# The two layers of a fused encoder trunk as a loop of two rounds, with the layer's number in a register

## What is computed

```python
def trunk_layer(x, pos, lw, lb, past):
    cq, ckv_raw, kr_raw, hq, hf, hi, hg, cu, cv, ga, gb, gc = jnp.split(x @ lw['w_in'], idx, axis=-1)
    ...   # A: latent attention; B: HGRN2 recurrence; C: gated MLP over chunks of 128 tokens
    m = jax.nn.sigmoid(ga) * y_a + jax.nn.sigmoid(gb) * y_b + jax.nn.sigmoid(gc) * y_c
    x = layer_norm(ALPHA * x + m @ lw['w_o'], lw['ln1_g'], lw['ln1_b'])
    gate, up = jnp.split(x @ lw['w_up'], 2, axis=-1)
    x = layer_norm(ALPHA * x + (jax.nn.silu(gate) * up) @ lw['w_down'], lw['ln2_g'], lw['ln2_b'])
    return x, (ckv, krope, S_fin, v_cm)
```

## Time and profile before

| | |
|---|---|
| median of 3 runs | 2124.44 us |
| lowest and highest | 2120.12, 2127.49 us |
| the profiled execution | 2126.03 us, its span 2124.2 us |
| TensorE busy | 2079.7 us, 98% |
| VectorE, ScalarE, GpSimd busy | 1175.1 us (55%), 713.6 us (34%), 82.7 us (4%) |
| mean granted TensorE clock | 0.987 of 2.4 GHz |
| DMA | 164.46 MB, mean 77 GB/s |

### The profile page before, as it was taken

The page is one execution under the profiler, slowest core; times in us unless marked ns, Lnnn a source line. Parts: engine busy times, 40 slices in busy tenths (PEclk is TensorE's granted clock), DMA queues, the critical chain, the costliest instruction groups (busy, mean ns, idle before and its releaser), DMA issues.

```text
span 2124.2 us, 38406 instructions
## 1 busy us (share of the span) xinstructions
PE 2079.7 (98%) x15974; PEld 1999.2 (94%) x15974; DVE 1175.1 (55%) x1886; ACT 713.6 (34%) x1154; POOL 82.7 (4%) x87
## 2 busy tenths in 40 slices
PE   7999999999999999999999999999999999999996
PEld 5899998898999999999989999989889999999996
DVE  5435645674376666654454366366725766666436
ACT  4232134444343232222343211354433432322224
POOL 1000001000010000000010000010000200000001
PEclk9999999999999999999999999999999999999997
DMA  5232213221132233322233222132213232332231
GB/s 168 80 81 54 67 44 84 70 62 51 51 109 80 79 89 89 87 84 83 85 90 81 70 61 72 43 93 57 66 31 100 80 89 80 89 89 81 85 93 52
DMA packets 288147, 164.46 MB, mean 77 GB/s; under 512 B 8712, under 2 KB 279280, under 8 KB 288016
## 3 DMA queue, kind: packets, MB, share of 16 engines
q1 hardware_dynamic: 284368, 153.11, 25.7%
q0 software_dynamic: 3168, 8.33, 1.3%
q10 hardware_dynamic: 480, 1.13, 0.2%
HBM read 157.88 MB, written 4.66 MB: 77 GB/s over the span
## 4 chain that ended last, share of the span: by engine, by line
PE 95%; DVE 3%; ACT 1%; issue 0%; DMA 0%; DVEq 0%; ACTq 0%
PE acc L669 51%; PE acc L655 25%; PE ring L689 4%; PE ring L773 2%; PE ring L916 2%; PE ring L935 1%; PE acc L689 1%; PE ring L924 1%; PE ring L986 1%; PE ring L968 1%; PE ring L1138 1%; PE ring L810 0%; PE ring L800 0%; DVE y L1807 0%; PE ring L903 0%; PE ring L824 0%
## 5 line engine op out<-in xcount | busy, mean ns | idle before, releaser
L1299 ACT ACTIVATE whi<-raw 128x1024 fp32r<-128x1024 f32 (+6 forms) x342 | 314.2, 919 | 751.7 <-PE acc L669 422.4
L1807 DVE TENSOR_TENSOR wlo<-raw,whi 128x1024 fp32r<-128x1024 f32 (+6 forms) x342 | 357.3, 1047 | 298.3 <-ACT whi L1299 297.0
L669 PE MATMUL acc<-xh,whi 128*128 128x272 f32 x1440 | 324.9, 307 | 2.9 <-DVE tmp L1807 2.6
L669 PE MATMUL acc<-xh,wlo 128*128 128x272 f32 x1440 | 300.2, 290 | 0.0
L669 PE MATMUL acc<-xl,whi 128*128 128x272 f32 x1440 | 299.9, 290 | 0.0
L655 PE MATMUL acc<-xh,whi 128*128 128x274 f32 (+1 forms) x1408 | 294.4, 290 | 0.0
L655 PE MATMUL acc<-xh,wlo 128*128 128x274 f32 (+1 forms) x1408 | 292.6, 289 | 0.0
L655 PE MATMUL acc<-xl,whi 128*128 128x274 f32 (+1 forms) x1408 | 292.2, 289 | 0.0
L669 PEld LDWEIGHTS acc<-xh,whi 128*128 128x128 f32 x1440 | 229.1, 191 | 18.7 <-issue 13.8
L669 PEld LDWEIGHTS acc<-xl,whi 128*128 128x128 f32 x1440 | 229.1, 190 | 0.0
L669 PEld LDWEIGHTS acc<-xh,wlo 128*128 128x128 f32 x1440 | 228.2, 190 | 0.0
(11 more groups left out here) (373 smaller groups left out, 3120.2 us busy)
## 6 DMA issues: line engine op xcount, KB each, us to landing
raw<-in_w_in_dram SPq DMA_DIRECT2D x106, 512.0 KB, 3.7
raw<-in_w_up_dram SPq DMA_DIRECT2D x88, 512.0 KB, 3.7
raw<-in_w_down_dram SPq DMA_DIRECT2D x32, 512.0 KB, 3.8
raw<-in_w_o_dram SPq DMA_DIRECT2D x16, 512.0 KB, 3.8
raw<-in_w_down_dram SPq DMA_DIRECT2D x16, 384.0 KB, 3.3
raw<-in_w_pc_dram SPq DMA_DIRECT2D x16, 256.0 KB, 2.8
raw<-in_w_pb_dram SPq DMA_DIRECT2D x16, 256.0 KB, 2.8
raw<-in_w_pa_dram SPq DMA_DIRECT2D x16, 256.0 KB, 2.8
```

Source lines behind the costliest of these rows:

```text
L669: last = pe.matmul(dst[:, b * 512:b * 512 + HALF], w[:, c:c + P], x[:, k0 + a, b * HALF:(b + 1) * HALF], start=start and a == 0 and q == 0 ...
L1299: return act.activation(dst, src, ACT.Copy)
L1807: return dve.tensor_tensor(out, a, b, op)
```

## The change

Every engine's walk over the layers becomes a loop on the chip with two rounds, whose counter `l` is a register. The body is built once. What depends on `l` (the wait values, the addresses of weights and outputs, the column of `lbcol`) is worked out by register instructions. The lines that count a semaphore's events in the first layer alone, and the reset of TensorE's buffer numbers, go, since the body is written only once. The norm keeps its place. In the changed file the lines stand about 10 higher: L1299 is L1288 there, L1807 is L1796, L689 is L679, L816 is L806.

```diff
-    first_layer = [True]
-
-    def layers():
-
-        for l in range(DEPTH):
-            first_layer[0] = l == 0
-            yield l
-        first_layer[0] = True
-
     def inc(name, times=1):
-        if first_layer[0]:
-            used[name] = used.get(name, 0) + times
+        used[name] = used.get(name, 0) + times
         return S_(name), (16 if name in DMA_SEMS else 1)
...
-        for l in layers():
+        with sp.Fori(0, DEPTH) as l:
             for n in range(2, 4):
                 load(l, U_CV + n, raw3(n, 2, 512), w_in[l, :, 2 * n:2 * n + 2, C_CV:C_CV + 512])
...
-        for l in layers():
-            ngroup[0] = ntile[0] = 0
+        with pe.Fori(0, DEPTH) as l:
             token_major(l, U_CV, "cv")
...
-        for l in layers():
+        with act.Fori(0, DEPTH) as l:
             for n in range(1, 4):
                 next_hi(l, n + 1)
...
-        for l in layers():
+        with dve.Fori(0, DEPTH) as l:
             dve.wait_ge(S_("lb_max"), 4)
...
-        for l in layers():
+        with pool.Fori(0, DEPTH) as l:
```

## The result

The changed kernel took 2131.94 us (median of 11 runs, 2128.18 to 2138.57), the kernel before 2124.70 us (median of 11 runs, 2120.12 to 2130.47). The ratio is 1.0035, with a 95% interval of 1.0022 to 1.0049: slower by 0.35%, where 2131 us had been forecast. The profiled execution took 2133.86 us, its span 2132.3, which is 8.1 us longer than the span before.

The account below looks back on a forecast made before the run. TensorE, busy 2079.7 of 2124.2 us, was taken to bound the kernel. Register form 0.5, new wait 3.2 and lower clock 2.5 made +6.2 us on the 2124.4 median: 2131 us, range 2124 to 2140 (8 in 10).

Parts of the forecast that it names:

- B: Layer border: ScalarE's jump back (3.0 us) and added table load (1.28 us) make TensorE wait 3.2 us at its third unit.
- the prediction's sign: ScalarE's trace shows a hole of about 3 us behind the last `xh` copy, then table load, then high part.
- rival 1: Layer border: jump hidden, ScalarE's program running ahead or block still held; 2125.6 us, not slower; chance 0.12.
- What the prediction called hidden: Layer border: TensorE's jump within its 3.8 us idle gap, VectorE's before unit 2's high part; SyncE, GpSimd delays covered.
- rival 4: Layer border: instruction fetch takes 5 to 7 us, adding +2 to +4 us, 2133 to 2136; chance 0.08.
- C: Behind the new wait at the third unit: TensorE's clock falls to its lower level, +2.5 us, from 0 to 5.1.
- A: Inside both layers: waits and addresses from registers change 22 hops ending TensorE's waits, +0.5 us, from -1.3 to +2.2.

Follow-up runs that it names:

- the last experiment: Kernel before, both layers written out, second layer leaving out the splits only a next layer needs: 2117.37 us against 2124.18, ratio 0.9971.

## Why the prediction was right

**B, the jump: right in kind and size.** ScalarE's jump was taken for 3.0 us and measured 2.8 to 2.9 (the changed kernel, and ScalarE alone in the loop); the chain to the third unit was worked out as a wait of 3.2 us and measured 3.4. Idle ScalarE was for 2.1 us only, where the prediction's sign was a hole of about 3: its 3.0 us count from the start of the last copy. That the wait came so near is in part luck, since two small errors nearly cancel: from the start of the last `xh` copy to the third unit it took 6.5 us in place of 6.7, and TensorE was ready for it after 3.1 us in place of 3.5. Three runs tie it to the far jump: the short loop (0.51 us a round), ScalarE alone (same hole, an instruction packet inside it), and the unit moved ahead of the jump (wait gone).

The rule of the Trainium skill, "Runtime: NRT & Kernel Launch", instruction fetch, on a taken branch to a page that isn't held, agrees with that. The queue rule behind rival 1, from the Trainium skill, "Advanced Engine Details and Errata", queue depths, didn't hide the jump. The instruction packet starts 1.0 us after the start of the last `xh` copy in the changed kernel (at 1075.98), not two copies sooner, since each of these copies waits for the norm. With unit 2's copy in between it starts 1.1 us after the same copy. So the part of rival 1 by which ScalarE's program runs ahead of its work is true, but only up to the next wait that isn't met.

What the prediction called hidden was hidden: on TensorE (its gap didn't grow), on SyncE and GpSimd. On VectorE it was hidden behind ScalarE's chain only: by itself it makes a wait of 2.7 us. The prediction's price of 3.0 us implied 1.7 of it (1080.4 + 0.2 + 1.2 = 1081.8, against 1080.14), but its text didn't say so. (In rival 4, +4 us gives 2135 and not 2136; nothing hangs on it.)

**B, the table load: right, but of less weight than its 1.28 us.** Without it the wait fell by 0.5 us in the traces, since VectorE's jump comes next.

**C, the clock: right in kind, its size by luck.** Taken as 2.5 us, it was 2.7 in the profiled execution. But four traces have such a wait, of 2.7 to 4.0 us, and the six microseconds behind it show 0.52 in the changed kernel and the following in the others (ScalarE alone; all but ScalarE; no table load):

```profile
1079.40:1085.40 6.00, 6.00 (x19) 0.72 0.68 179
...
1080.70:1086.70 6.00, 6.00 (x26) 1.00 0.83 242
...
1080.50:1086.50 6.00, 6.00 (x26) 1.00 0.78 229
```

The two longer waits (3.4 and 4.0) were followed by low clock, the two shorter (2.7 and 2.9) not, and neither were the waits of 1.2 us of the table load alone and of the short loop. The loss was 2.7 us once, 1.7 once (0.28 of 6 us, ScalarE alone) and twice nothing. With one trace each it stays open whether the length decides it or where the wait falls against earlier low stretches. The runs of the changed kernel themselves aren't alike: four of the eleven show a mean granted clock of 0.988 and take 2128.2 to 2128.7 us, six show 0.985 and take 2131.5 to 2133.9 us.

**A, the register form: small, but over the term.** With TensorE, SyncE and GpSimd in it the ratio is 0.9991, with all five and the jump hidden 0.9998; the intervals reach from -0.22% to +0.14%, so the times can't tell A's 0.5 us from 0. The stream of the up loop is as before:

```profile
656.53 260.59 PE acc L645 x2058
```

The traces, matched matmul by matmul, show more than 0.5: TensorE falls back by 0.7 us in layer 0 (599 to 650) and 0.9 in layer 1 (1601 to 1690), the largest steps being at the first unit of `w_o` (0.2) and at the first up unit (0.3). It is 1.6 us together in the changed kernel and with the unit moved ahead as well, 1.4 with all but ScalarE in the loop, 0.4 with TensorE, SyncE and GpSimd in it, and 0.2 with ScalarE alone. So most of it needs VectorE's register form. 1.6 us is inside the range of -1.3 to +2.2, but not by its working: that had looked at hops that end TensorE's waits, and these lie at places where TensorE hadn't waited before.

**The sum.** 0.5 + 3.2 + 2.5 = 6.2 us was forecast. The medians differ by 7.2 us, and by 6.1 between the changed kernel and the one with the unit moved ahead, each against its own runs of before; that one is B and C, less what the useless split of the last round costs. In the two traces A 1.6, B 3.5 and C 2.7 make 7.8 of the 8.1 us. So the sum came right with A taken too low and C near by luck; the term that carries it, B, was right.

## What to carry to other kernels

Here a jump back over a whole layer cost ScalarE and VectorE about 3 us each, and a short one 0.5 us or less. So before you write such a loop, read on every engine what its first work in the body feeds, and how late that may be. Where it is short of 3 us, put one more unit of look-ahead in front of the jump; where two engines are short of it, both need that. The time counts from the last wait ahead of the jump that isn't met yet, and work behind that wait runs beside the jump, as ScalarE's did with the unit moved ahead. And ask what the last round does for a round that never comes: here that was worth as much as the jump.

## What the runs showed that I had not expected

- The price of the far jump hardly depends on how many engines jump: 2.9 us on ScalarE alone, 2.8 with all five; on VectorE 3.1 to 3.3 us, whether ScalarE jumps too or not. With the unit moved ahead VectorE's took 3.8 us (1076.63 to 1080.41); there its instruction packet started 1.4 us in and took 0.8 us, against 1.1 and 0.4 in the changed kernel. Why is open.
- A table load at a loop's head comes from the set that each way into the loop holds: with the square root's set on both ways the compiler left it out.
- How long TensorE waits for a late unit depends on its own clock before: the chain on the other engines was nearly the same, yet its wait was 3.4 us in the changed kernel and 4.0 with ScalarE alone in the loop. In the trace of the last experiment, whose border is that of the kernel before, TensorE waits 0.6 us at the third unit, where it had waited for nothing.
- Nearly the same waits in layer 0's attention (1.3 us both times) were followed by a clock of 0.66 over 15 us before and by 1.00 after, and in layer 1 the low stretch moved from 1404 to 1384. Single executions of one kernel thus differ by several us, and one pair of traces wouldn't have settled a change of 7 us.
